# A hybrid decoder step on one core: six of retention's cache slots placed behind it

## The reference

```python
h = _rmsnorm(x, norm1_w) * (1 + sc1) + sh1          # x: 512 x 1024 prompt, 32 x 1024 sample
z = h @ w_in                                        # 1024 -> 3584
rq, rk, rv, rg, mq, mk, mv = jnp.split(z, SPLITS, axis=-1)
ret_out, ret_s = _retention_branch(...)             # 8 heads of 64, in chunks of 128 tokens
moba_out = moba_mix(heads(mq), heads(mk), heads(mv))
x = x + g1 * (jnp.concatenate([ret_out, moba_out], axis=-1) @ w_out)
h2 = _rmsnorm(x, norm2_w) * (1 + sc2) + sh2
x = x + g2 * ((jax.nn.silu(h2 @ w_gate) * (h2 @ w_up)) @ w_down)    # 1024 -> 2816 -> 1024

# retention, for each chunk of 128 tokens
att = einsum('bhid,bhjd->bhij', qc, kc) * dmat
o = einsum('bhij,bhjv->bhiv', att, vc) + einsum('bhid,bhdv->bhiv', qc, s) * q_dec
s = s * c_dec + einsum('bhjd,bhjv->bhdv', kc * k_dec, vc)

# sample attention: the 16 blocks of 256 cached tokens are ranked by q . mean(k of the block),
# the best 3 and the new tokens attend; the pages come from cache_k, cache_v by a page table
k_sel = cache_k[phys, :, hi, :]; v_sel = cache_v[phys, :, hi, :]
```

## Time and profile before

| | us |
|---|---|
| median of the three runs | 1020.14 |
| the three runs | 1020.59, 1020.14, 1014.70 |
| the profiled execution, its own time | 1015.21 |
| its span on the core | 1013.4 |
| TensorE busy | 956.7 (94%) |
| VectorE busy | 600.8 (59%) |
| ScalarE busy | 335.4 (33%) |
| GpSimd busy | 141.3 (14%) |
| DMA | 269.13 MB, mean 266 GB/s |

### The profile page before, as it was taken

The page is one execution under the profiler, slowest core; times in us unless marked ns, Lnnn a source line. Parts: engine busy times, 40 slices in busy tenths (PEclk is TensorE's granted clock), DMA queues, the critical chain, the costliest instruction groups (busy, mean ns, idle before and its releaser), DMA issues.

```text
span 1013.4 us, 20844 instructions
## 1 busy us (share of the span) xinstructions
PE 956.7 (94%) x7951; PEld 678.5 (67%) x7951; DVE 600.8 (59%) x999; ACT 335.4 (33%) x722; POOL 141.3 (14%) x129
## 2 busy tenths in 40 slices
PE   3889999999999888989999999999999999999996
PEld 1567776766677555557766777676677777777775
DVE  1665765666566478986787684532565555454234
ACT  5411243344333435542252152432333222111113
POOL 0020113333200032215151240000000000000000
PEclk9999999999999999989999899999999999999999
DMA  9998778888776899979898678677475776777662
GB/s 339 374 352 276 273 274 297 307 254 278 274 256 219 303 372 336 400 267 295 326 340 311 199 281 258 228 242 226 134 231 164 249 228 229 237 241 240 218 208 89
DMA packets 172212, 269.13 MB, mean 266 GB/s; under 512 B 12769, under 2 KB 122665, under 8 KB 163922
## 3 DMA queue, kind: packets, MB, share of 16 engines
q1 hardware_dynamic: 88386, 127.70, 37.3%
q10 hardware_dynamic: 74512, 72.99, 22.3%
q0 software_dynamic: 9216, 67.11, 17.7%
HBM read 260.04 MB, written 5.64 MB: 262 GB/s over the span
## 4 chain that ended last, share of the span: by engine, by line
PE 75%; DMA 9%; DVE 8%; issue 2%; SPq 2%; DVEq 2%; ACT 1%; ACTq 0%
PE banks L1163 13%; PE banks L1164 12%; PE banks L1165 12%; PE banks L1116 6%; PE banks L1176 5%; PE banks L1251 5%; DMA K<-in_cache_k,kidx 4%; PE banks L1196 4%; PE banks L1178 4%; PE banks L1177 4%; DVE KT L1909 3%; PE banks L1375 2%; DMA ctr<-in_const 1%; DMA raw<-in_w_gate 1%; DMA rawm<-in_w_mod 1%
## 5 line engine op out<-in xcount | busy, mean ns | idle before, releaser
L678 ACT ACTIVATE whi<-raw 128x1024 fp32r<-128x1024 f32 (+1 forms) x76 | 78.6, 1034 | 273.9 <-PE banks L1165 237.0
L1909 DVE STREAM_TRANSPOSE KT<-K 128x2048 f32<-128x2048 f32 x63 | 145.5, 2309 | 33.5 <-PE banks L1196 14.9
L1163 PE MATMUL banks<-ahi,whi 128*128 128x512 f32 x400 | 163.4, 408 | 1.3 <-DVE rawlo L1872 1.2
L1164 PE MATMUL banks<-alo,whi 128*128 128x512 f32 x400 | 157.5, 394 | 0.0
L1165 PE MATMUL banks<-ahi,rawlo 128*128 128x512 f32 x400 | 156.9, 392 | 0.0
L1872 DVE TENSOR_TENSOR rawlo<-raw,whi 128x1024 fp32r<-128x1024 f32 (+1 forms) x76 | 92.1, 1212 | 59.4 <-ACT whi L678 56.4
L543 POOL DMA_INDIRECT K<-in_cache_k,kidx x64 | 64.5, 1008 | 388.4 <-DVE KT L1909 339.3
L1163 PEld LDWEIGHTS banks<-ahi,whi 128*128 128x128 f32 x400 | 75.7, 189 | 31.1 <-issue 13.0
L1176 PE MATMUL banks<-ahi,whi 128*128 128x512 f32 x216 | 89.4, 414 | 1.2 <-DVE rawlo L1879 0.9
L1165 PEld LDWEIGHTS banks<-ahi,rawlo 128*128 128x128 f32 x400 | 75.8, 190 | 16.7
L1164 PEld LDWEIGHTS banks<-alo,whi 128*128 128x128 f32 x400 | 76.0, 190 | 14.1
(11 more groups left out here) (340 smaller groups left out, 1498.3 us busy)
## 6 DMA issues: line engine op xcount, KB each, us to landing
V<-in_cache_v SPq DMA_DIRECT2D x168, 256.0 KB, 4.9
zT<-in_cache_v SPq DMA_DIRECT2D x56, 256.0 KB, 5.1
raw<-in_w_in ACTq DMA_DIRECT2D x12, 1024.0 KB, 7.8
rawm<-in_w_mod ACTq DMA_DIRECT2D x11, 1024.0 KB, 8.7
raw<-in_w_gate ACTq DMA_DIRECT2D x11, 1024.0 KB, 5.4
raw<-in_w_up ACTq DMA_DIRECT2D x11, 1024.0 KB, 5.4
srw<-in_w_gate SPq DMA_DIRECT2D x11, 1024.0 KB, 7.7
srw<-in_w_up SPq DMA_DIRECT2D x11, 1024.0 KB, 5.2
```

Of the source, the lines that this page charges most:

```text
L678: act.activation(whi[t % 2][:, 0:kd, :], raw[u][:, 0:kd, t % 2 * P:(t % 2 + 1) * P], ACT.Copy).then_inc(s_hi, 1)
L1163: pe.matmul(out[:, :], whi[t % 2][:, k, :], hi(k), start=(first and n == 0), stop=False)
L1164: pe.matmul(out[:, :], whi[t % 2][:, k, :], lo(k), start=False, stop=False)
L1909: dve.transpose(KTb[:, :, :, :], Kb[g % 2][:, :]).then_inc(s_kt, 1)
```

## The change

Steps and tiles stay where they are. Steps 30 to 42 held thirteen slots; now they hold seven (slots 30 to 36), two for each of the first three head pairs and one for the fourth. From step 43 on a step takes the keys of slot `s - 6`: keys end at step 69 and values at step 81. Four of the eight transpositions of x move out of retention to output tiles 1 to 4. In retention, VectorE makes the states before the next key transposition, and the chain of sequence 3 (`B_RET`) has places of its own there. The second norm loses the special places of a sequence's maxima and exponentials (`B_NORM`). The value ring in the second key buffer is gone: even slots 26 to 48 have rings 2 and 3, and all slots from 49 on share ring 0. SyncE starts slot 16's values before slot 18's. The sample's stages begin six steps later; to fit, its output chunks come two a step (steps 84 and 85), and of the gate and up chunks 0 and 1, 6 and 7, 12 and 13 share a step, and the product of a pair is made at the end of VectorE's step.

```diff
-B_NORM = R_NORM // NGRP - 1
+BEHIND = 6
+SLOT_IN_RET = {R_PAIR: 30, R_PAIR + 1: 31, R_PAIR + 3: 32, R_PAIR + 4: 33, R_PAIR + 6: 34, R_PAIR + 7: 35, R_PAIR + 9: 36}
+slot_of = lambda step: step if step < R_PAIR else SLOT_IN_RET.get(step) if step < R_OUT else step - BEHIND
+B_RET = 3
-S_END = NG + LAG
-S_OUT, S_NORM, S_FFN = S_END + 2, S_END + 6, S_END + 8
-S_DOWN = S_FFN + FT
+S_END = NG + LAG + BEHIND
+S_OUT, S_NORM, S_FFN = S_END + 2, S_END + 4, S_END + 6
+S_CHUNKS = []
+for _chunk in range(FT):
+    if _chunk in (1, 7, 13):
+        S_CHUNKS[-1] += (_chunk,)
+    else:
+        S_CHUNKS.append((_chunk,))
+chunks_at = lambda i: S_CHUNKS[i] if 0 <= i < len(S_CHUNKS) else ()
+S_DOWN = S_FFN + len(S_CHUNKS)
-RING_2 = {17: 7, 18: 1, 20: 5, 21: 1, 23: 5, 24: 1, 26: 1, 27: 5}
+RING_2 = {17: 7, 18: 1, 20: 5, 21: 1, 23: 5, 24: 1}
-RING_2.update({g: 2 if g < 32 else 3 if g < 53 else 4 for g in range(29, NG, 2)})
+RING_2.update({g: 2 if g < 30 else 3 for g in range(26, 49, 2)})
...
SyncE:
-        for g in [RING_FROM, RING_FROM + 1, RING_FROM - 1] + list(range(RING_FROM + 2, NG)):
+        for g in [RING_FROM, RING_FROM - 1] + list(range(RING_FROM + 1, NG)):
-            if g == 29:
+            if g == 26:
                 sp.wait_ge(s_ra, HP)
-            if g == 33:
+            if g == 30:
                 sp.wait_ge(s_hlo, 2 * KT)
-            if g == 53:
-                sp.wait_ge(s_kt, NG)
...
GpSimd, retention:
+        next_keys(30)
+        next_keys(31)
+        next_keys(32)
+        queries_decayed(0)
+        next_keys(33)
...
+        next_keys(34)
+        for hp in range(1, HP):
+            queries_decayed(hp)
+            if hp >= 2:
+                scale_heads(hp - 2)
+            next_keys(33 + 2 * hp)
+            if hp < HP - 1:
+                next_keys(34 + 2 * hp)
+        scale_heads(HP - 2)
...
ScalarE (and, alike, TensorE and VectorE):
-        def slot(s):
+        def slot(step):
+            s = slot_of(step)
+            if s is None:
+                return
...
-                act.wait_ge(s_vd, 4 * 27)
+                act.wait_ge(s_vd, 4 * 25)
                 next_chunk(0)
-                keep_x(5)
...
+            if 1 <= f <= 4:
+                keep_x(3 + f)
...
TensorE, the sample:
-            if 0 <= c < 4:
+            for c in (2 * (s - S_OUT), 2 * (s - S_OUT) + 1) if 0 <= s - S_OUT < 2 else ():
                 pe.wait_ge(s_sev, N_OUT + c + 1)
                 streamed(c, (DB, VO)[c % 2], lambda k: asT[:, k, :])
...
+            for q in chunks_at(s - S_FFN - 1):
+                if q % 2:
+                    turn_hidden(q // 2)
+            for q in chunks_at(s - S_FFN):
+                pe.wait_ge(s_sev, N_FFN + q + 1)
+                streamed(4 + q, (VO, DB)[q % 2], lambda k: asT[:, k, :])
...
VectorE, retention:
             slot_rest(s)
+            decayed(hp)
             if hp:
                 variance(hp - 1)
-            decayed(hp)
             slot_head(s + 1)
+            if hp == 2:
+                row_max(B_RET)
+                exp_bias(B_RET)
+            states(hp)
             slot_rest(s + 1)
-            states(hp)
+            if hp == 1:
+                select(B_RET)
...
VectorE, the sample:
-                if n % 2:
-                    sample_product(n // 2)
+            for q in chunks_at(s - S_FFN - 1):
+                sample_fold(q)
...
+            for q in chunks_at(s - S_FFN - 1):
+                if q % 2:
+                    sample_product(q // 2)
```

More of the change, by code:

```diff
@@ L596, in _, with next_keys @@
         gather(1)
-        for g in range(2, NG):
+        def next_keys(g):
             pool.wait_ge(s_kt, g - 1)
             gather(g)
+        for g in range(2, R_PAIR):
+            next_keys(g)
             if M_TURN <= g - 4 < M_TURN + 2 * HP:
@@ L1000, in norm_hi @@
             act.activation(ahi[:, k, :], zT[:, k, :], ACT.Identity, bias=mT[:, 24 + k, NB_SEQ:NSEQ]).then_inc(s_hhi, 1)
-        norm_hi(0)
-        norm_hi(1)
-        keep_probs(B_NORM, 1)
-        for k in range(2, KT):
+        slot(R_NORM + 1)
+        for k in range(KT):
             norm_hi(k)
+        slot(R_NORM + 2)
         def sample_silu(pair):
@@ L2362, in sample_first @@
                 dve.wait_ge(s_xs, 32)
-            if 0 <= s - S_OUT - 1 < 4:
-                c = s - S_OUT - 1
+            for c in (2 * (s - S_OUT) - 2, 2 * (s - S_OUT) - 1) if 1 <= s - S_OUT <= 2 else ():
                 dve.wait_ge(s_ss, N_OUT + c + 1)
```

181 lines of the change are left out of this document (88 added, 93 removed).

## The result

The changed kernel took 1046.78 us (median of four runs, 1042.51 to 1054.87) against 1017.42 us for the kernel before (four runs): ratio 1.0297, 95% interval 1.0253 to 1.0342. It is 3% slower. Forecast was 1011 us.

What follows compares the result with a forecast made beforehand. Retention was taken as held by its slots, with TensorE full behind it. Terms: -26 + 2.4 + 12 + 2 - 1.5 - 3 + 2.5 + 4.5 = -7.1 us, from the 1018.5 mean 1011 us; range 1000 to 1025.

Steps and rivals of the forecast that it cites:

- What bounds the kernel: Retention is held by its slots, about 5.9 us each; behind it TensorE is full, each microsecond it gets costing one.
- Retention: Stage from 356.6 to 441.8 us: six slots fewer bring it to 59 us, -26 (bounds 53 to 70).
- 1 for clock: In retention: 1 us added for TensorE's clock in the sum that gives 59 us.
- the two kinds that I named: In retention: TensorE's waits for VectorE's states and for key transpositions, 1 us on each of eight, 8 us.
- The rival of the used-up gain: Retention's chain, not the slots, sets 68 us: -17 instead of -26, sum +1.9, 1020 us; chance 0.2.
- The ring: Steps 70 to 81: values share one ring, pages come late, 0.2 us a step: +2.5 us (bounds 0 and 8).
- The sample: Output chunks and gate and up pairs, two a step, make TensorE wait: +4.5 us (bounds 1 and 9).
- The norm: Second norm, 514.3 to 541.2: some 1.8 us of VectorE's work leaves, -1.5 us (bounds 0 and -2.7).
- Step 28: Slot 16's values start about 4 us earlier; the wait and most of the slow stretch go: -3 us (bounds 0 and -5).
- the transpositions of x: Four of them now stand in output tiles, where TensorE is busy: +2.4 us.
- the slots' price: Behind retention: six slots' keys and values at 2.0 us each on TensorE, +12 us.
- The clock: Rival: TensorE falls to its lower level more often, half of retention's work there, retention 78 us, 1030 us in all; chance 0.1.

Runs made afterwards that it cites:

- the kernel of 1031.6 us: Changed kernel with a value ring for slots 54 to 60, slot 24 in ring 0, two extra sample buffers, early x load, one-sequence state store: 1031.6 us.
- the second ring: Changed kernel with even slots 54 to 60 given a value ring in the second key buffer once all keys are used: 1043.76 us.
- the pairs alone: Kernel before, with only the sample's output chunks two a step and three pairs of gate and up chunks sharing steps: 1021.76 us, ratio 1.0056.
- the small store: Changed kernel whose store of the sample's state writes only the first of eight sequences, 512 pieces instead of 4096: 1042.82 us.

## Why the prediction was wrong

- *What bounds the kernel* was right behind retention: TensorE is full there, and a slot's keys cost 1.0 us (6.1 us for six). That retention was held by its slots fits the rows, but no run tested it on the kernel before, and six slots fewer gave 12.7 us, not 26. (The 11.5 us for two slots make 5.75 us a slot, not 5.9.)
- *Retention* is the step that failed most, -12.7 us instead of -26: "I put 1 us on each of the eight waits: 50 + 8 = 58, and 1 for clock". The waits were 17.9 us, not 8: the two kinds that I named came to 9.4, and 8.5 more were for ScalarE's copies and a sequence's small chain, which I had at nothing. Beside them "1 for clock" was 7 to 8 us by the estimate above, and the work at the higher level 46 to 47 instead of 50. The two key buffers still make a loop of gather and transposition, and of the 59 I named, 59.5 is what remains when six gathers and six transpositions are taken away altogether: I had costed a chain in which they are hidden, and the work that had hidden them, the slots' own matmuls, was what the change removed (I read this from the two profiles; no run put such matmuls back). ScalarE's wait for the output weights was overlooked: I asked of VectorE what ends last, and not of ScalarE. The rival of the used-up gain had retention at 68, which is what the profile shows of the kernel of 1031.6 us (356.28 to 424.47); its reason, that the slots' matmuls no longer cover the waits, fits the runs without gathers and transpositions, but it had the costs behind as small as the forecast.
- *The ring* was 9 us in the kernel before and 5 to 7 in the changed one, where I had +2.5 with a bound of 8. The fourth page was asked for 5.1 us after the values' start, as forecast (717.42 against 712.32), but I took 3.0 us to its landing, the shortest of the earlier trace rows, and its matmuls began 3.9 us after the issue (721.31): 1.6 us late, not 0.7. A late step does give the next one more time, but the step behind that one is late again: steps 73, 75, 77 and 79 took 7.9 to 9.3 us, and 6.7 to 7.1 with the second ring. My 0.2 a step left that out. (And before, it was the odd slots that had another ring, not the even ones.)
- *The sample* was 14.5 us (14.9 + 3.9, less the 4.3 us of work that only moved there) instead of 4.5. I let chunk 3's load be 1 us late. The loads of a pair can start only when the chunks before it have been used, at the end of a step, and with the prompt's own weights that is 3 MB in a 6 us tile; the step was 5 us over. In steps 83 to 96 TensorE waited 7.6 us in all (4.0 for output chunks, 2.9 for `asm`, 0.6 for an up chunk), and behind these waits it was busy for 9.6 us at the lower level of its clock, where before it had none: an estimate of 4 to 5 us, in no term of mine (the rows are below). That 6 us came back in the pairs alone (at the end, where the sample had ended) is not to be had when the sample starts six steps later.

```profile
799.24:806.07 6.83, 6.18 (x26) 4.13 (x27) 5.14 (x12) 1.19 (x3) 0.00 (x0) 0.50 0.89 297
833.37:836.79 3.42, 3.42 (x18) 2.15 (x7) 2.26 (x5) 0.41 (x1) 0.00 (x0) 0.50 0.38 112
```

- *The norm* was +4.7 instead of -1.5. I counted what leaves VectorE there and not what arrives: VectorE's work rose from 32.4 to 35.6 us in the stretch; new in it are the sums of the next sequence and the copies of its queries. TensorE waited there 2.2 us for transposed keys (0.6 before) and 2.9 for `ahi` (2.1 before), and was busy 2.2 us longer at a granted clock of 0.92 (0.95 before). Which of VectorE's pieces made the keys late stays open.
- *The store* was in no term. It cost 2.5 us in steps 64 to 69 of this profile (51.1 against 48.6 with the small store). I had not asked which transfers, already under way, the moved steps would meet.
- *Step 28* (-2.3 against -3), the transpositions of x (+1.5 against +2.4) and the slots' price were about right.
- *The clock.* Retention's granted clock fell from 0.92 to 0.86. TensorE was busy at the lower level for 16.7 of 54.5 us, under a third and not half, and the rival's retention of 78 us did not come. Against before it costs 2 us more there, and 6 to 7 in the whole program, where such busy time rose from 33 to 47 us; these are estimates from the trace, and no run changed the clock alone. My 6 us for it in the kernel before were right by luck: of the two slow groups that I named, the values at 406.02 ran at a granted clock of 1.00.

Of +35.2 us in the profile against -7.1 forecast, 42 in all: retention 13, the sample 10, steps 70 to 82 8 (3 to 5 of them the ring), the norm 6, steps 55 to 63 3, the store 2 to 3, and the rest in small pieces. What lengthened steps 55 to 63, and the rest of steps 70 to 82, was not looked into. Whether the norm's 5 us could be had back by another order stays open: only one move was tried.

## What to carry to other kernels

When work is taken out of a stage, ask what it had been hiding there: the gain is the stage's new chain with every two-buffer loop still in it, not its busiest engine. When work is put behind, list every transfer and every engine that already is at that place, and add their demands slice by slice; a store in small pieces that was free beside nothing is not free beside gathers. When a page's time to landing enters a sum, take the range that the rows show, not its shortest value.

## What was not expected of the hardware

- A load of 128 KB issued behind a store of 4096 pieces of 256 bytes held ScalarE's instruction stream for 8.8 us in the kernel before (9.8 and 10.0 in two variants of it), and for 11.3 to 19.1 us in five profiles where key gathers ran beside it. Issued ahead of the store it took 0.99 us, and behind a store of 512 such pieces 0.52 us.
- One instruction of VectorE stood still for 5.7 us (a 32x32 copy of 0.17 us) or 5.6 us (a 128x512 low part of 0.74 us) while GpSimd ran four products in 4.99 us; its neighbours took their usual time.
